# Up-projection of a streaming encoder layer: products in another order, one summed on another in PSUM, operands prepared one block earlier

## The reference, cut to what matters

```python
x   = x + rmsnorm(concat(A, B) @ w_out, g_attn_post)
xn  = rmsnorm(x, g_ffn_pre)
u   = xn @ w_up                      # 1024 -> 5632
c   = conv_b + sum(ext[:, k:k+t] * conv_w[k] for k in range(3))
h   = gelu(gate of c) * (value of c)
x   = x + rmsnorm(h @ w_down, g_ffn_post)
```

## Time and profile before

| what | us |
|---|---|
| median of 3 runs | 2662.8 |
| the profiled execution, whole | 2663.3 |
| its span (first to last instruction) | 2661.2 |
| output projection, last block | 1147.6 to 1185.4 of the span |
| quad 0 (with the wait ahead of it) | 1185.4 to 1230.1 |
| quads 1 to 21 | 1230.1 to 1661.7 |
| quad 22 | 1661.7 to 1703.0 |
| quads 23 to 43 | 1703.0 to 2133.1 |
| down-projection | 2133.1 to 2661.2 |

### The profile page before, as it was taken

How to read it: one execution, slowest core, us unless ns; L and a number is a source line. 1 busy time by engine, 2 the same in 40 slices (tenths; PEclk the granted TensorE clock), 3 DMA queues, 4 the chain that set the end, 5 groups by cost and what they waited for, 6 DMA issues and landing times.

```text
span 2661.2 us, 42677 instructions
## 1 busy us (share of the span) xinstructions
PE 2550.3 (96%) x15719; PEld 2354.6 (88%) x15719; DVE 1957.8 (74%) x2585; ACT 1284.9 (48%) x2475; POOL 469.6 (18%) x367
## 2 busy tenths in 40 slices
PE   8999978899999998988999999799999999999997
PEld 7999955677777878988999999799999999999997
DVE  6877668788878854999888886888888754465454
ACT  5444258567666764445444433444444444344242
POOL 1111041244334433440000000000000011111111
PEclk9999989899999999999999999899999999999999
DMA  7666656444444524564432335322222354645633
GB/s 217 224 225 219 199 177 181 101 82 83 81 77 78 96 75 161 182 215 167 171 109 87 101 99 183 127 78 83 73 81 78 117 206 163 233 167 186 232 132 120
DMA packets 222657, 376.89 MB, mean 142 GB/s; under 512 B 56692, under 2 KB 159828, under 8 KB 220628
## 3 DMA queue, kind: packets, MB, share of 16 engines
q1 hardware_dynamic: 222452, 374.23, 45.6%
HBM read 269.37 MB, written 105.57 MB: 141 GB/s over the span
## 4 chain that ended last, share of the span: by engine, by line
PE 72%; DVE 6%; ACT 2%; issue 2%; POOL 2%; SPq 1%; DMA 1%; DVEq 0%; ACTq 0%; POOLq 0%
PE mf_ps L2496 32%; PE mf_ps L2519 17%; PE at_ps L1643 7%; PE mf_ps L2435 5%; PE at_ps L1629 2%; PE at_ps L1661 2%; PE at_ps L1664 2%; PE at_ps L1662 2%; DVE la_part L1743 1%; POOL mf_area L2397 1%; ACT wa_prob L1142 1%; DVE la_low L1441 1%; DMA room<-in_w_out 0%; DVE mf_rounded L2908 0%; ACT mf_rounded L2765 0%
## 5 line engine op out<-in xcount | busy, mean ns | idle before, releaser
L2496 PE MATMUL mf_ps<-mf_rounded,mix_rest_rounded 128*128 128x264 f32 x4752 | 676.5, 285 | 10.5 <-DVE mf_rounded L2908 10.5
L2496 PEld LDWEIGHTS mf_ps<-mf_rounded,mix_rest_rounded 128*128 128x128 f32 x4752 | 621.8, 189 | 11.6 <-issue 8.3
L2519 PE MATMUL mf_ps<-mf_rounded,mix_rest_rounded 128*128 128x424 f32 (+1 forms) x2616 | 504.9, 354 | 0.0
L2519 PEld LDWEIGHTS mf_ps<-mf_rounded,mix_rest_rounded 128*128 128x128 f32 x2616 | 490.6, 188 | 12.3 <-issue 1.3
L3023 DVE TENSOR_TENSOR mix_rest_rounded<-mf_area,mix_rest_rounded 128x1408 fp32r<-128x1408 f32 x80 | 129.9, 1623 | 247.2 <-ACT mix_rest_rounded L2750 247.2
L2496 PE MATMUL mf_ps<-mf_rounded,mf_rounded 128*128 128x264 f32 x1584 | 284.4, 288 | 8.0 <-DVE mf_rounded L2908 4.2
L1643 PE MATMUL at_ps<-ahead_q,ahead_k 96*128 96x512 f32 (+8 forms) x1008 | 259.3, 366 | 0.0
L2750 ACT ACTIVATE mix_rest_rounded<-mf_area 128x1408 fp32r<-128x1408 f32 x80 | 110.5, 1381 | 306.6 <-PE mf_ps L2519 304.1
L1700 ACT ACTIVATE la_prob<-at_ps 128x512 f32<-128x512 f32 (+1 forms) x336 | 175.5, 522 | 155.9 <-PE at_ps L1643 140.1
L2397 POOL TENSOR_TENSOR mf_area<-mf_area 128x424 f32<-128x424 f32 (+1 forms) x97 | 155.6, 1604 | 507.0 <-ACT mf_area L2553 367.5
L2496 PEld LDWEIGHTS mf_ps<-mf_rounded,mf_rounded 128*128 128x128 f32 x1584 | 232.8, 192 | 9.0 <-issue 8.6
(11 more groups left out here) (248 smaller groups left out, 4639.8 us busy)
## 6 DMA issues: line engine op xcount, KB each, us to landing
mf_area<-in_w_down SPq DMA_DIRECT2D x80, 704.0 KB, 4.1
mix_rest<-in_w_up SPq DMA_DIRECT2D x168, 256.0 KB, 3.0
pi_w_raw<-in_w_in SPq DMA_DIRECT2D x49, 512.0 KB, 6.3
h_scr<-mf_area SPq DMA_DIRECT2D x22, 528.0 KB, 3.5
h_scr<-mf_area SPq DMA_DIRECT2D x22, 496.0 KB, 3.3
mf_area<-h_scr SPq DMA_DIRECT2D x8, 1060.0 KB, 6.6
la_rec_all<-inv_scr SPq DMA_DIRECT2D x32, 256.0 KB
ahead_k<-kn_scr SPq DMA_DIRECT2D x28, 280.0 KB, 5.1
```

The costliest lines, as they stand in the source:

```text
L2496: mm = pe.matmul(pair[slots[i]][:, e], w[:, k], x[:, e * HB:(e + 1) * HB], start=(k == 0 and m == 0 and i < 6), stop=(k == KH - 1 and m == 2),
L2519: mm = pe.matmul(acc[:, t % 2, 0:n], w[:, half, k], x(b, kk)[:, 0:n], start=(kk == 0 and e == 0), stop=(kk == KF - 1 and e == 2))
```

## The change

1. Order of products: B11, T2, T3, T1, T4, B21, B22. The product with B22 starts on top of the one with T1 in its PSUM pair, as the one with B21 does on B11. `mix_right` (two additions) goes; each quad increments `mixed` five times, not six. The pairs' roles rotate over three quads.
2. Opening: the fourth block's residual, squares and norm leave the last projection block and join the late chain, which has 16 tiles (two a quad, quads 1 to 4 and 6 to 9, then 11 to 14 and 16 to 19) and three norm sums (quads 0, 6, 12). Their y is kept in `yo_scr`. Group 0's sums, rounding and low parts go into that block. T3 is made from the B22 tile that T2 uses, so it no longer waits for the separate B22.
3. Change of groups: `change_of_groups` puts the token operands ahead of quad 21's convolution and gating, and the fetch of quad 23's kept weights goes behind all operand loads.
4. Convolution and gating: in group 1 both halves follow in the next quad. `mix_upper_right` waits for the last product and stands at the head of the next quad's list, and at the end behind `h_low` of 0 to 2.

```diff
-        B11, T2, T3, T4, T1, B22, B21 = range(PRODUCTS)
+        B11, T2, T3, T1, T4, B21, B22 = range(PRODUCTS)
...
+        def sums_of(q):
+            return u_other if q >= KF and q % 2 == 0 else u_first
+        def slots_of(q):
+            return ((2, 1, 3, 0), (3, 1, 0, 2), (0, 1, 2, 3))[q % 3]
...
+        LATE = [(c, j) for c in (LAST - 1, LAST) for j in range(KD)]
...
-        LATE_NORM = (0, KD + 2)
+            return [t for t in range(len(LATE)) if q == (KD + 3 if t < KD else KD + 4) + t // 2]
+        LATE_NORM = (0, 6, 12)
+        LATE_ROOT = (5, 10, 15)
...
             sp.wait_ge(chunk_done, KD * LAST)
+            load_left(0, B11, 0, 0)
             keep_xn(LAST - 2, 1)
-            load_left(0, B11, 0, 0)
+            sp.wait_ge(xn_out[0], 64)
+            load_right(0, T3, 1, 0)
+            load_right(0, T2, 2, 1)
             sp.wait_ge(chunk_done, KD * LAST + 2)
             for x in (A21, A22, A11, A12):
                 load_weights(0, x)
...
+            keep_yo(LAST - 1)
             sp.wait_ge(chunk_done, KD * LAST + 5)
             load_left(0, T4, 3, 1)
             sp.wait_ge(chunk_done, KD * LAST + 7)
-            load_right(0, B22, 4, 1)
-            keep_xn(LAST - 1, 0)
+            load_left(0, B21, 5, 1)
             sp.wait_ge(chunk_done, OC)
-            load_left(0, B21, 5, 1)
             for x in (A21, A22, A11, A12):
                 load_weights(1, x)
...
+            keep_yo(LAST)
+            load_right(0, B22, 4, 1)
...
-                if q + 2 in BACK:
-                    fetch_weights(q + 2, 0)
                 if turn:
                     load_right(1, T3, 1, 0)
+                if q + 2 == BACK[0]:
+                    fetch_weights(q + 2, 0)
...
+                if q > KF + 2:
+                    keep_h(q - 1)
+                sp.wait_ge(chunk_done, product(q, 5))
+                if nxt:
+                    load_weights(q + 2, A12)
+                if turn:
+                    load_left(1, B21, 5, 1)
...
+                if q + 2 == BACK[1]:
+                    fetch_weights(q + 2, 0)
+                    fetch_weights(q + 2, 1)
+                if KF <= q <= KF + 2:
+                    keep_h(q - 1)
...
-                slots = (first, 1, 2, spare, 1, 2, first)
+                slots = (first, left, second, right, left, first, right)
...
-                    if i == 3 and q:
-                        pe.wait_ge(corner_kept, q)
+                    if i == 3:
+                        pe.wait_ge(corner_kept, q) if q else pe.wait_ge(evacuated, OC)
                     if i == 4:
-                        pe.wait_ge(mixed, 6 * q + 1)
+                        pe.wait_ge(mixed, 5 * q + 1)
                     if i == 5:
-                        pe.wait_ge(mixed, 6 * q + 2)
+                        pe.wait_ge(first_kept, q + 1)
                     if i == 6:
-                        pe.wait_ge(first_kept, q + 1)
+                        pe.wait_ge(mixed, 5 * q + 3)
...
-                    if b == LAST and j == 5:
+                    if b == LAST and j == 2:
+                        x_round(0, B11)
+                    if b == LAST and j == 3:
                         up_weights(0, 0)
                         up_weights(0, 1)
+                    if b == LAST and j == 4:
+                        x_round(0, T2)
+                    if b == LAST and j == 5:
+                        x_round(0, T3)
                     if b == LAST and j == 6:
-                        x_round(0, B11)
+                        x_round(0, T1)
+                        x_round(0, T4)
...
             x_sums(0, T1)
+            x_sums(0, T3)
+            sums(0, 0)
+            sums(0, 1)
+            x_sums(0, T2)
             x_low(0, B11)
-            x_sums(0, T2)
+            up_weights(0, 0)
+            up_weights(0, 1)
             x_sums(0, T4)
-            x_low(0, T2)
-            x_sums(0, T3)
+            for i in (T2, T3, T1, T4):
+                x_low(0, i)
...
-                dve.wait_ge(chunk_done, product(q, 5))
-                dve.wait_ge(mixed, 6 * q + 4)
-                dve.tensor_tensor(right(0, s), pair[2], right(0, s), ALU.add).then_inc(mixed, 1)
+                dve.wait_ge(chunk_done, product(q, 6))
+                dve.wait_ge(mixed, 5 * q + 4)
+                dve.tensor_tensor(right(0, q), pair[slots_of(q)[3]], right(0, q), ALU.add).then_inc(mixed, 1)
...
+            def change_of_groups(q):
+                for i in (T2,):
+                    x_low(1, i)
+                mix_upper_right(q - 1)
+                x_low(1, T3)
+                x_low(1, T1)
+                mix_first(q)
+                x_low(1, T4)
+                mix_second(q)
+                x_low(1, B21)
+                mix_lower_right(q)
+                x_low(1, B22)
+                mix_lower_left(q)
+                conv(q - 1, 1)
+                conv(q - 1, 0)
+                glu(q - 1)
...
+            for q in range(KF):
+                next_quad(q)
+            x_low(1, B11)
+            x_sums(1, T3)
+            x_sums(1, T2)
+            x_sums(1, T4)
+            change_of_groups(KF)
+            for q in range(KF + 1, QUADS):
+                next_quad(q)
+            for k in range(3):
+                h_low(0, k)
+            mix_upper_right(QUADS - 1)
```

More of the change, by code:

```diff
@@ L1881, in mix_and_ffn @@
                 T1: tuple(("area", 8976 + SW * k) for k in range(KH)),
[L1882 to L1883 removed]
+                B21: (("area", 11088), ("area", 11616), ("rest", 11264), ("rest", 11792)),
+                B22: tuple(("area", 33488 + SW * k) for k in range(KH))}
         H_LATER = (35608, 35608 + TB)
@@ L2711, in _, with late_square, chain_then_first @@
-            for q in range(QUADS):
-                s = q // KF
+            def late_square(t):
+                c, j = LATE[t]
+                n = cols(c)[1]
+                act.wait_ge(x1_made, KD * c + j + 1)
+                act.activation(late_y[t % 2][:, 0:n], late_x[t % 2][:, 0:n], ACT.Square).then_inc(sq_made, 1)
+            def chain_then_first(q):
                 if q:
                     corner_out(q - 1)
+                    if q > KF:
+                        tap(q - 1, 1)
                     tap(q - 1, 0)
+                first_out(q)
@@ L2716, in _ @@
                 if q == 0:
-                    x_round(0, T2)
-                if q % KF == 0 and s:
-                    x_round(s, T3)
-                first_out(q)
-                if q:
+                    x_round(0, B21)
+                if q and q <= KF:
+                    gelu(q - 1)
+            for q in range(QUADS):
+                more = q + 1 < QUADS and q + 1 not in BACK
+                if q == KF:
+                    x_round(1, T2)
+                    x_round(1, T3)
+                    first_out(q)
+                    corner_out(q - 1)
+                    x_round(1, T1)
+                    x_round(1, T4)
+                    tap(q - 1, 0)
+                    x_round(1, B21)
+                    x_round(1, B22)
+                    gelu(q - 1)
+                elif KF < q <= KF + 2:
+                    first_out(q)
+                    corner_out(q - 1)
+                else:
+                    chain_then_first(q)
+                if more:
+                    up_weights(q + 1, 0)
+                    up_weights(q + 1, 1)
+                if KF < q <= KF + 2:
+                    tap(q - 1, 1)
+                    tap(q - 1, 0)
+                if q > KF:
@@ L2961, in mix_second @@
                 dve.wait_ge(chunk_done, product(q, 2))
-                dve.wait_ge(mixed, 6 * q + 1)
+                dve.wait_ge(mixed, 5 * q + 1)
                 if q == 0:
-                    dve.wait_ge(yo_out, 32)
-                dve.tensor_tensor(right(1, s), pair[2], right(0, s), ALU.add).then_inc(mixed, 1)
-            def mix_lower_left(q):
-                s, spare = q // KF, 0 if q % 2 else 3
-                dve.wait_ge(chunk_done, product(q, 3))
-                dve.wait_ge(mixed, 6 * q + 2)
+                    dve.wait_ge(yo_out, 64)
@@ L3029, in h_low, with next_quad @@
                                   ALU.subtract).then_inc(h_split, 1)
-            for q in range(QUADS):
-                s, first, turn, last = q // KF, q % KF == 0, q == KF - 1, q == QUADS - 1
-                more = q + 1 < QUADS and q + 1 not in BACK
-                if first:
-                    x_low(s, T3)
+            def change_of_groups(q):
[14 more added lines that the diff above has]
+                glu(q - 1)
+            def next_quad(q):
+                if q:
+                    mix_upper_right(q - 1)
+                more, late_chain = q + 1 < QUADS and q + 1 not in BACK, KF < q <= KF + 2
                 if more:
                     sums(q + 1, 0)
-                if q:
+                if q > KF + 2:
+                    conv(q - 1, 1)
+                if 0 < q < KF:
                     conv(q - 1, 0)
-                if first:
-                    x_low(s, T4)
```

412 lines of the change are left out of this document (211 added, 201 removed).

## The result

The changed kernel takes 2640.85 us (median of 4 runs, 2637.4 to 2643.2) against 2663.2: a ratio of 0.9915, 95% interval 0.9901 to 0.9930. The forecast was 2635, with 2621 to 2651 for the range. So the direction and the likeliest case came true, and the time came out 6 us above the forecast.

The account below looks back on a forecast made before the run. TensorE bounds the kernel, never idle mid-stage, with 45.0 us lost in quads 0 and 22. 19.6 + 10.0 - 0.5 - 0.6 - 0.8 = 27.7 us off 2663.3 gives 2635.6, median 2635; range 2621 to 2651.

Parts of the forecast that it names:

- opening: Last projection block and quad 0: quad 0 ends at 1210.5 against 1230.1, 19.6 us won, bounds 9 to 24.2.
- change of groups: Quad 22: B12 lands 4 us sooner, TensorE waits 6.6 us for T2; 10.0 us won, bounds 4 to 15.
- third norm sum: On TensorE: one more norm sum for the late chain costs 0.6 us.
- late quads: Quads with two late tiles: VectorE 18.5 of 20.5 us busy, barely covered; 0.5 us lost, bounds 0 and 5.
- quads 23 to 43: Second group's ordinary quads: 20.5 us a quad and clock 1.00, no change in time.
- end: Start of the down-projection: TensorE waits at the twelfth low part of h; 0.8 us lost, bounds 0 and 2.
- waits for `mixed` or `first_out` in ordinary quads: Sign in ordinary quads' TensorE waits that would show the prediction wrong; no size given.
- (a): Opening: B12, B22 and weights land ten us later, holding the seventh product 13 us; 2650 in all; chance 0.14.
- (b): Quads 0 and 22: nearly all 45.0 us go, as loads come early and sums keep ahead; 2620; chance 0.09.
- (c): From quad 25: first tap waits for a late h store, 2.3 us in each of 19 quads; 2679; chance 0.07.
- (d): 16 late quads: quad 0's 20 us return as waits, 1.7 each, VectorE needing over 22 us; chance 0.03.
- one slow product a quad: Rotating PSUM pairs drops the clock: 2.3 us in 42 quads, 97 us, 2732 in all; chance 0.02.

Follow-up runs that it names:

- three edits: Changed kernel with ScalarE's upper tap ahead of late squares, upper convolution behind `mix_upper_right`, and quad 43's `mix_upper_right` behind h's low parts: 2632.6 us, 0.9886 of before.
- weights behind: Changed kernel with ScalarE rounding quad 0's weight parts behind the last block's fifth copy, not its fourth: 2639.7 us, 0.9922 of before.
- tap and mix ahead: Changed kernel with ScalarE's upper tap ahead of the late squares and VectorE's upper convolution behind `mix_upper_right`: 2636.7 us, 0.9907 of before.
- tap or mix ahead: Two runs on the changed kernel: ScalarE's upper tap ahead of late squares, 2634.8 us; or VectorE's upper convolution behind `mix_upper_right`, 2635.8 us.

## Why the prediction was near, and the step that failed

The forecast was 27.7 us of gain within the execution; 19.85 were there. By its steps, each stage counted from the last matmul of the stage ahead of it to its own last one:

| step | forecast | measured | from |
|---|---|---|---|
| opening (block and quad 0) | 19.6 | 18.0 | 83.0 to 65.0 |
| change of groups (quads 21, 22) | 10.0 | 10.9 | 61.92 to 51.07 |
| third norm sum | -0.6 | -0.5 | quads 6 and 12 are 0.7 longer each, where quad 10 of before was 1.0 longer |
| late quads | -0.5 | -7.7 | quads 1 to 20: 410.7 to 418.9, less the norm sum |
| quads 23 to 43 | 0 | +0.4 | 430.1 to 429.7 |
| end | -0.8 | -1.2 | 528.1 to 529.3 |

That the median came within 6 us of the forecast is in part luck: by the stages alone (2662.8 less 19.85) it would have been 2643, and the 2.5 us more lie outside everything that the forecast dealt with.

**The late quads are the step that failed**, sized at "0.5 us for the late quads, bounds 0 and 5"; 7.7 is outside even the bounds. Two sentences of the working were wrong. One is "The upper right mix goes to the next quad's head, is done 2 us in, and is needed at 5.9": in quad 2 it was done 7.5 us in (1235.58 less 1228.1). The other is that the late chain "ends 2 to 3 us into the next quad: covered, barely", by VectorE's work of 18.5 us in 20.5. The sum of work was nearly right: with three edits, both orders mended, quads 1 to 20 take 412.0 us, and less the norm sum that is 0.8 above before, against the 0.5 that I took. What was not asked is in which order the chain runs over two engines. Two squares that each wait for VectorE stand ahead of a tap that VectorE waits for, and the mix was moved behind that wait: a sum of durations on one engine does not see that engine standing still. The wait itself was there to be read in the trace of before (1.49 us, above). The sign that the prediction named for being wrong, "waits for `mixed` or `first_out` in ordinary quads", did appear. The 4.8 us of waits cost more than their length, too: each of the eight quads lost about 0.4 us beside its idle time. Of that, 0.16 is the overlap that neighbouring matmuls otherwise have, and most of the rest are slower starts behind the wait and a short delay at the fifth product.

**The opening** was right in its mechanism: the hold was forecast as "some 3 us", ended by ScalarE's copy, and was 3.6; no wait in quad 0 was over 3 us. It was 1.6 short: B12 was taken 18.4 us behind the block's start and came at 19.7, and VectorE's sharing with GpSimd, taken as 1.5 us, was over 4: T1's sum took 3.30 (2.36 at the change of groups), two of B11's low parts 2.20 (1.32), the weights' second low part 3.18 (2.28), T2's low parts 3.33 (2.56), the twelve that follow 8.39 (three times 2.5). Part of that had slack. The clock of the seventh product was not in the forecast (0.80 behind the hold), and by the run with the weights behind it costs nothing: only VectorE's list counts.

**The change of groups** came out as written: one wait of 6.4 us for T2 (forecast 6.6), quad 22's end 10.9 us sooner, counted from the end of quad 20. Its parts were tried one at a time: fetches 3.8 us (forecast 4), the lagging convolution 8.1. That they sum to more than 10.9 would fit with the three sums now ahead of T2 costing part of it; that order itself wasn't undone, so this is not shown.

**The end** was 1.2, within 0 to 2, and the wait came at the twelfth low part, as written.

**The rivals.** (a), late transfers: B12 was 1.3 us late, not ten. (b), all 45 us: quads 0 and 22 still take 1.8 and 10 us over 20.5 (quad 22 with the wait ahead of it), and the block 4.8 more than before. (c), slower in group 1 by a late store: quads 23 to 43 took 429.7 with 429.70 busy. (d), the late quads: the place was right, the size under half (8 of 20), and its reason wrong; VectorE did not need 22 us a quad, it needed another order. The rule of the Trainium skill on cycling through PSUM banks (TensorE: Matmul & The Clock Gate, A second HAM failure mode: psum-queue depth-cycling) would, as the prediction read it, have cost one slow product a quad; the granted clock is 1.00 in both long stretches.

## What to carry to other kernels

When work is added to an engine that has slack, don't compare sums of work alone: write the two or three engines' lists beside each other, and look for an instruction that waits for the other engine and stands ahead of one that the other engine waits for. Read the idle times of the engines with slack in the trace of before as well: one that costs nothing there costs its length once something that TensorE needs is queued behind it. Put what TensorE needs (here a mix of 0.7 us) ahead of anything that waits, whatever else is late. A hold on TensorE that comes ahead of a still longer list on another engine costs nothing, and mending it gains nothing, until the list gets shorter.

## What the runs showed of the hardware

The same hold in the last block, 3.0 to 3.8 us, was followed by a granted clock of 0.80 over the next 8.6 us in eight traces, and by 1.00 in one, that with tap and mix ahead, though its hold was 3.2 us:

```profile
1178.25:1186.85 8.60, 8.60 (x37) 8.40 (x38) 8.60 (x5) 7.21 (x15) 4.54 (x3) 0.80 0.10 26
```
```profile
1178.27:1186.87 8.60, 8.60 (x45) 8.48 (x46) 8.60 (x5) 7.97 (x16) 5.24 (x3) 1.00 0.29 90
```

The first is of the version with three edits, the second of that with tap and mix ahead: 37 matmuls against 45 in the same time. After the hold of 1.1 to 1.35 us of the four versions with the weights behind it was 1.00 each time. Why one of nine long holds escaped is open; a gap of that size is a risk of the lower level and no certainty.

VectorE's slowing beside one GpSimd addition was 0.7 to 0.9 us for several forms: a two-input pass over 1056 columns took 2.04 in place of 1.32 us, T1's sum over 2112 columns 3.30 in place of 2.36. T4's sum, from 1180.34, took its usual 2.34; there it was GpSimd's addition beside it that took 3.03 us, where others took 1.08. The Trainium skill (Advanced Engine Details and Errata, Mode Summary) says that VectorE's second port is shared with GpSimd, so that GpSimd's instructions and VectorE's two-port ones block each other; the trace agrees that they collide, and can't show whether that port is why. And a wait is no more than its place in a queue: the Trainium skill's Perfetto Trace Analysis (Tensor Engine Instruction (MATMUL, LD_WEIGHTS)) calls VectorE and ScalarE strictly first in, first out, and the runs with tap or mix ahead agree: moving one instruction ahead of another that waits gave back 4.8 to 5.7 us with no work removed.
